# Recurrence of an encoder layer: order of ScalarE's copies, and the state update in two halves

## The reference

```
b = cumsum(log f); state = exp(b_last) * state + (k * exp(b_last - b))^T v
o = (scores of q and k, decayed, lower triangle) v + (q * exp(b)) state
```

## Time and profile before

| what | value |
|---|---|
| median of 3 runs | 1780.27 us (1780.04 to 1784.52) |
| profiled execution | 1780.42 us |
| its span in the trace | 1778.6 us, mean granted clock 0.991 |
| the eight heads | 283.1 to 657.7 us of the span |
| increments of head 1 to increments of head 2 | 46.84 us |

### The profile page before, as it was taken

How to read it: one execution, slowest core, us unless ns; L and a number is a source line. 1 busy time by engine, 2 the same in 40 slices (tenths; PEclk the granted TensorE clock), 3 DMA queues, 4 the chain that set the end, 5 groups by cost and what they waited for, 6 DMA issues and landing times.

```text
span 1778.6 us, 23518 instructions
## 1 busy us (share of the span) xinstructions
PE 1690.8 (95%) x9625; PEld 840.3 (47%) x9625; DVE 598.2 (34%) x942; ACT 331.8 (19%) x512; POOL 136.8 (8%) x141
## 2 busy tenths in 40 slices
PE   6999999999999999999999999999999999898967
PEld 3444455555555555556555554533333333333323
DVE  5010128888888863100112786300000000000008
ACT  1111112222222221112000220022222121121212
POOL 0000000000000000000000111511111111111100
PEclk9999999999999999999999999999999999999989
DMA  6114101110111001111117006699999999999848
GB/s 222 47 48 165 49 24 36 37 35 26 33 35 35 13 1 50 56 47 36 53 53 290 24 36 247 237 422 422 422 425 422 422 423 421 414 411 405 336 197 354
DMA packets 104986, 330.51 MB, mean 186 GB/s; under 512 B 8496, under 2 KB 64848, under 8 KB 86736
## 3 DMA queue, kind: packets, MB, share of 16 engines
q1 hardware_dynamic: 91520, 291.69, 41.5%
q0 software_dynamic: 13392, 37.77, 5.4%
HBM read 306.88 MB, written 33.55 MB: 191 GB/s over the span
## 4 chain that ended last, share of the span: by engine, by line
PE 77%; DMA 12%; DVE 6%; ACT 2%; issue 2%; SPq 0%; POOL 0%; DVEq 0%; POOLq 0%; ACTq 0%
PE pA L1055 14%; PE pg L679 11%; PE pg L706 9%; PE pg L838 9%; PE pB L1081 6%; PE pB L869 5%; DMA rA<-w_e_gate_up 4%; PE pg L719 2%; PE pB L918 2%; PE pA L918 2%; PE pA L861 2%; DMA rCD<-w_e_gate_up 2%; DMA rEF<-w_e_gate_up 2%; DMA rA<-y_dram 2%; DMA rB<-w_e_gate_up 2%
## 5 line engine op out<-in xcount | busy, mean ns | idle before, releaser
L706 PE MATMUL pg<-rA,hw 128*128 128x384 f32 x768 | 264.5, 493 | 0.7 <-ACT aTr L1191 0.7
L1055 PE MATMUL pA<-rCD,aTr 128*32 128x512 f32 (+2 forms) x720 | 209.1, 600 | 11.1 <-DMA rA<-w_e_gate_up 10.1
L679 PE MATMUL pg<-rEF,rA 128*128 128x512 f32 x448 | 194.7, 596 | 3.1 <-ACT rCD L1170 3.1
L1788 DVE TENSOR_TENSOR rows<-rows,pA 128x256 f32<-128x256 f32 x45 | 18.9, 421 | 530.8 <-ACT rows L1314 530.8
L706 PEld LDWEIGHTS pg<-rA,hw 128*128 128x128 f32 x768 | 140.2, 190 | 86.5 <-ACT aTr L1191 0.9
L838 PE MATMUL pg<-rA,hw 128*128 128x384 f32 x512 | 165.3, 486 | 0.0
L679 PEld LDWEIGHTS pg<-rEF,rA 128*128 128x128 f32 x448 | 85.5, 192 | 109.6 <-issue 109.6
L838 PEld LDWEIGHTS pg<-rA,hw 128*128 128x128 f32 x512 | 97.2, 190 | 67.6
L1055 PE MATMUL pA<-rA,aTr 128*32 128x512 f32 (+2 forms) x384 | 124.2, 606 | 0.3 <-DMA rB<-w_e_gate_up 0.3
L1081 PE MATMUL pB<-rCD,rows 128*32 128x512 f32 (+2 forms) x360 | 106.8, 605 | 2.0 <-DMA rCD<-w_e_down 2.0
L1055 PE MATMUL pA<-rB,aTr 128*32 128x512 f32 (+1 forms) x368 | 106.0, 594 | 2.0 <-DMA rEF<-w_e_gate_up 2.0
(11 more groups left out here) (326 smaller groups left out, 2159.6 us busy)
## 6 DMA issues: line engine op xcount, KB each, us to landing
rCD<-w_e_gate_up SPq DMA_DIRECT2D x21, 2048.0 KB, 30.6
rA<-w_e_gate_up SPq DMA_DIRECT2D x11, 2048.0 KB, 31.3
rB<-w_e_gate_up SPq DMA_DIRECT2D x11, 2048.0 KB, 29.6
ew<-w_e_gate_up SPq DMA_DIRECT2D x11, 2048.0 KB, 33.3
rEF<-w_e_gate_up SPq DMA_DIRECT2D x11, 2048.0 KB, 33.0
rCD<-w_e_down SPq DMA_DIRECT2D x21, 1024.0 KB, 33.0
hw<-w_in SPq DMA_DIRECT2D x40, 512.0 KB, 3.9
rA<-w_e_down SPq DMA_DIRECT2D x11, 1024.0 KB, 31.6
```

The source lines that it names most:

```text
L679: last = mm(big_bank(fill), x1T[:, c, i * P:(i + 1) * P], strip[n % 2][:, c, :], start=(c == 0), stop=(c == KC - 1))
L706: last = mm(pg[:, n * 512:n * 512 + HALF], hw3[m][:, c, :], x1T[:, c, n * HALF:(n + 1) * HALF], start=(c == 0), stop=(c == KC - 1))
L1055: last = mm(gu[n][o:o + w, :], xT[n][:, c, o:o + w], at(gate_up_home(j % NB)[0], gate_up_home(j % NB)[1] + c * F, [[2 * D, 2], [1, F]]), s ...
L1788: v.tensor_tensor(hid[n], silu_g[n], gu[n][:, F:2 * F], ALU.mult).then_inc(h_ready, 1)
```

## The change

The transposes and the increments get semaphores of their own (`kt_filled`, `inc_filled`), raised after 4 of 8 tiles and after 8, so that `FILLS` falls from 11 to 9. The decayed keys, the eviction of the transposes and the states are each split in a forward and a backward half. In ScalarE's queue the middle and near copies move ahead of the far ones, and all of them ahead of evict 4.

```diff
-FILLS = 11
+FILLS = 9
...
 def k_transposed():
-    pe.wait_ge(ke_ready, 2 * h + 1)
     for s in range(8):
+        if s % 4 == 0:
+            pe.wait_ge(ke_ready, 3 * h + (s // 4 + 1))
...
-    last.then_inc(hg_filled, 1)
+        if s % 4 == 3:
+            last.then_inc(kt_filled, 1)
 def increments():
-    pe.wait_ge(ke_evicted, h + 1)
     for s in range(8):
+        if s % 4 == 0:
+            pe.wait_ge(ke_evicted, 2 * h + (s // 4 + 1))
...
+        if s % 4 == 3:
+            last.then_inc(inc_filled, 1)
...
 # ScalarE, one head
-for x in range(5): evict(x)
+for x in range(4): evict(x)
 sc.wait_ge(hg_filled, h * FILLS + LEVELS)
 ... middle copies
-sc.wait_ge(hg_filled, h * FILLS + (LEVELS + 1))
-... far copies
 sc.wait_ge(hg_used, h * USES + USES)
 sc.wait_ge(mid_taken, 2 * h + 2)
 ... near copies
-sc.wait_ge(hg_filled, h * FILLS + 9)
-fn(keT, slabs(pair[0][:, :], 8), ACT.Copy).then_inc(ke_evicted, 1)
+sc.wait_ge(hg_filled, h * FILLS + (LEVELS + 1))
+... far copies
+evict(4)
+for a in range(2):
+    half = slice(4 * a * P, 4 * (a + 1) * P)
+    sc.wait_ge(kt_filled, h * 2 + (a + 1))
+    fn(keT[:, 4 * a:4 * a + 4, :], slabs(pair[0][:, half], 4), ACT.Copy).then_inc(ke_evicted, 1)
...
 # VectorE, one head
-v.tensor_tensor(hv("S", 2), hv("S", 2), hv("k", 2), ALU.mult).then_inc(ke_ready, 1)
+for a in range(2):
+    o = slice(a * T, (a + 1) * T)
+    v.tensor_tensor(hv("S", 2)[:, o], hv("S", 2)[:, o], hv("k", 2)[:, o], ALU.mult).then_inc(ke_ready, 1)
...
-ve.wait_ge(hg_filled, h * FILLS + 10)
-corners = [[4 * P, 2], [3 * P, 2], [1, P]]
-link(v.tensor_copy(at(ew, 8 * P, corners), at(pair[1], 0, corners)))
-for s in (1, 2, 5, 6):
+for a in range(2):
+    ve.wait_ge(inc_filled, h * 2 + (a + 1))
+    ends = [[3 * P, 2], [1, P]]
+    link(v.tensor_copy(at(ew, (8 + 4 * a) * P, ends), at(pair[1], 4 * a * P, ends)))
+    for s in (4 * a + 1, 4 * a + 2):
```

More of the change, by code:

```diff
@@ L409, in build @@
         ke_evicted = sem("k_transposed_in_sbuf")
+        kt_filled = sem("k_transposed_in_psum")
+        inc_filled = sem("state_increments_in_psum")
         far_taken = sem("far_scores_in_sbuf")
@@ L788, in increments @@
                                   start=True, stop=True)
-                    last.then_inc(hg_filled, 1)
+                        if s % 4 == 3:
+                            last.then_inc(inc_filled, 1)
                 def outputs():
                     buf = start(10)
-                    pe.wait_ge(ke_ready, 2 * h + 2)
+                    pe.wait_ge(ke_ready, 3 * h + 3)
                     pe.wait_ge(st_ready, h + 1)
@@ L1204, in head @@
                 sc.wait_ge(cur_taken, h + 1)
-                for x in range(5):
-                    evict(x)
                 def scores_out(src, w, g, to):
@@ L1210, in scores_out @@
                               slabs(src[g * w:(g + 1) * w, 0:NT * w], NT), ACT.Copy)
+                for x in range(4):
+                    evict(x)
                 sc.wait_ge(hg_filled, h * FILLS + LEVELS)
@@ L1214, in head @@
                     scores_out(pair[(LEVELS - 1) % 2], HB, g, g).then_inc(mid_taken, 1)
-                sc.wait_ge(hg_filled, h * FILLS + (LEVELS + 1))
-                for g in range(2):
-                    scores_out(pair[LEVELS % 2], HB, g, 1 - g).then_inc(far_taken, 1)
                 sc.wait_ge(hg_used, h * USES + USES)
@@ L1221, in head @@
                     scores_out(near, QB, g, g).then_inc(near_taken, 1)
-                sc.wait_ge(hg_filled, h * FILLS + 9)
-                fn(keT, slabs(pair[0][:, :], 8), ACT.Copy).then_inc(ke_evicted, 1)
+                sc.wait_ge(hg_filled, h * FILLS + (LEVELS + 1))
+                for g in range(2):
+                    scores_out(pair[LEVELS % 2], HB, g, 1 - g).then_inc(far_taken, 1)
+                evict(4)
[3 more added lines that the diff above has]
+                    fn(keT[:, 4 * a:4 * a + 4, :], slabs(pair[0][:, half], 4), ACT.Copy).then_inc(ke_evicted, 1)
                 evict(5)
@@ L1226, in head @@
                     clear_suffixes()
-                sc.wait_ge(hg_filled, h * FILLS + 11)
+                sc.wait_ge(hg_filled, h * FILLS + FILLS)
                 fn(o_tok[:, :, bass.ds(h * DK, DK)].rearrange("p (a b) k -> p a b k", a=2),
@@ L1521, in head @@
                         ve.wait_ge(hg_used, h * USES + (j + 1))
-                v.tensor_tensor(hv("S", 2), hv("S", 2), hv("k", 2), ALU.mult).then_inc(ke_ready, 1)
-                ve.wait_ge(ke_ready, h * 2 + 1)
+                for a in range(2):
+                    o = slice(a * T, (a + 1) * T)
+                    v.tensor_tensor(hv("S", 2)[:, o], hv("S", 2)[:, o], hv("k", 2)[:, o], ALU.mult).then_inc(ke_ready, 1)
+                ve.wait_ge(ke_ready, h * 3 + 2)
                 v.tensor_tensor(slabs(hv("k", 2), 2), at(rEF, OFF["q"], [[0, 2], [1, T]]),
                                 slabs(hv("P", 2), 2), ALU.mult).then_inc(ke_ready, 1)
-                ve.wait_ge(hg_filled, h * FILLS + 10)
-                corners = [[4 * P, 2], [3 * P, 2], [1, P]]
-                link(v.tensor_copy(at(ew, 8 * P, corners), at(pair[1], 0, corners)))
-                for s in (1, 2, 5, 6):
[L1531 to L1537, removed]
+                for a in range(2):
[3 more added lines that the diff above has]
+                    for s in (4 * a + 1, 4 * a + 2):
+                        i = FWD_TILES[s] if s < 4 else BWD_TILES[s - 4]
+                        edge = i * P + P - 1 if s < 4 else T + i * P
+                        last = v.scalar_tensor_tensor(out=states[:, s, :], in0=states[:, s - 1, :],
+                                                      scalar=hv("P", 2)[:, edge:edge + 1],
+                                                      in1=pair[1][:, s * P:(s + 1) * P], op0=ALU.mult, op1=ALU.add)
+                        if s < 6:
+                            link(last)
                 last.then_inc(st_ready, 1)
```

## The result

The changed kernel takes 1772.32 us (median of 5 runs, 1770.77 to 1774.3), against 1780.27 for the kernel before in the same comparison (5 runs, 1779.96 to 1784.52). The medians differ by 7.95 us. The ratio, which goes by all of the runs, is 0.9949, with an interval of 0.9939 to 0.996: 9.1 us faster, between 7.1 and 10.9. The profiled execution took 1770.77 us, with a span of 1768.9. The sum of the prediction was 10.2 us and 1770.2 for a profiled execution.

The account below looks back on a forecast made before the run. TensorE was taken to bound the kernel (77% of the chain), with some 3 us of each 46.84 us head in waits. 7 x 1.37 + 0.57 = 10.2 us off 1780.42 gave 1770.2 profiled, 1770.1 median; range 1766.5 to 1776.5.

Parts of the forecast that it names:

- The circle: Between heads: L1491 waits for the outputs and starts the next head, so earlier outputs shorten a head equally, 1.37 us.
- Keys: Transposes to increments: keys evicted earlier let increments follow the products without a wait, saving 0.60 us (0.52 to 0.70).
- States: Increments to outputs: the forward half of the states overlaps the backward increments, saving 0.77 us a head.
- Edits costed at nothing: Split decayed keys, TensorE's two added waits and evict 4 behind the far copies: each taken to cost or gain 0.
- VectorE's cover behind the outputs: VectorE's idle time before L1491, waiting for the outputs: shrinks from 1.24 to 0.95 us and holds.
- Only the eviction gains: Rival: states still end with the whole increments; a head saves 0.60, the last nothing; 1776 us; chance 0.09, shared.
- The new waits cost more: Rival: TensorE's waits inside transposes and increments cost 0.76 each, more than the gain; 1782 us; chance 0.08, including something unseen.
- Issue stays: Rival: TensorE's wait ahead of the outputs is its own issue and stays; 1776 us; chance 0.09, shared.
- The dearer half: Rival: a half of VectorE's copy and states takes 1.44 us, not 1.20; 6.1 us gained, 1774.3; chance 0.05.
- everything behind the heads shifts and gives nothing back: After the last outputs: later work starts from their end on TensorE's queue, so all 10.2 us reach the whole time.

## Why the prediction was right

*The circle.* L1491 did wait for the outputs in each head, and the head became shorter by what the outputs were earlier: 45.43 against the 45.5 predicted.

*Keys.* 0.60 was reckoned for increments that follow the products without a wait; it was 0.68. TensorE's overlap with the last product was taken too small: the increments start 0.17 ahead of its end (403.80 + 1.46 = 405.26 against 405.09), where 0.09 was put in.

*States.* 0.77 was reckoned, 0.72 measured (4.51 to 3.79). A copy of 256 columns takes 0.42, as interpolated, and a half 1.19 against 1.20. What came out longer is the step from the forward half to the backward one: 1.31 us from copy to copy, not 1.23, though the backward increments are done by 405.09 + 1.95 = 407.04, and the copy starts at 407.49. VectorE stands idle 0.12 us ahead of it instead of 0.03. In the last head, which stands behind VectorE's loop, the same two copies are 1.23 apart. So the hand-over is dearer inside the loop; no run shows why. The first copy, 1.09 behind the increments' start and not 1.14, made up for part of it. And only 0.62 of the 0.72 is the overlap of states and increments, as the states alone show; 0.10 comes from increments that are no longer held, and belongs to the earlier keys.

The two errors cancel, and that is luck: 0.08 more for the keys, 0.05 less for the states, 1.41 a head in place of 1.37. In the last head 0.70 came in place of 0.57, since its outputs follow 0.10 behind the states and not 0.20, before as after. The wait that stays ahead of the outputs is 0.55, not 0.4: the products beside it start 1.78 behind the increments' start, not 1.89, for the first matmul is no longer the long one.

*Edits costed at nothing.* The split keys were worth nothing, shown by the run with whole keys. TensorE's waits cost nothing, shown with 12 more of them. (The price from which they would have eaten the gain is not 0.69 a wait, as the rival has it, but 0.64 over all heads: 10.2 us over 16 waits.) Evict 4 started as its product ended, behind the far copies, with 0.48 to spare. VectorE's cover behind the outputs was predicted to shrink from 1.24 to 0.95; it is 1.17.

*The rivals.* "Only the eviction gains" falls with the halves alone, worth 0.62 a head. "The new waits cost more" falls with the wait ahead of each tile. "Issue stays" falls with the 0.20 between states and outputs, in heads 1 to 6 of every trace. The dearer half falls with the rows: a state follows the copy within 0.04 us, two take 0.73, and a head saves 1.41, not 0.86. That is against the rule of the Trainium skill that was weighed ("VectorE: DVE Perf Modes", section "The DRAIN you can't avoid"), by which a pause of 0.16 would stand there: the measurement decides. The same section adds that an operation which is not held starts earlier, without a size, and so leaves room for what the rows show. The profiled execution took 1770.77, against 1774 by the rule; the median, 1772.32, lies between the two sums and would not have told them apart.

*Where it missed.* It treated order and eviction in halves as one saving and did not see that either alone gives 0.50 or 0.53 of 0.68. It took it that everything behind the heads shifts and gives nothing back. The median came out 2.2 us above 1770.1, so 7.95 us of 10.35 arrived. In the traces this lies in the part behind the heads (1121.7 to 1124.7), of which the execution underlying the sum was among the shortest (1121.0). That term of the sum is not confirmed.

## What to carry to other kernels

When a loop's stages close a circle over several engines, find the instruction that starts the next round and reckon each edit by how much earlier it comes; the sum over rounds was within 2% of the shift of the last outputs here, in part because two errors cancelled, and the whole time gained less than that shift. An eviction stands behind whatever its queue holds: moving small copies into time in which their engine waits anyway, or splitting the eviction, works on the same wait, and one of them alone took about two thirds of it (0.50 or 0.53 of 0.78 us, the held start counted in). Once the tail is shorter, look again at where the filler work stands: moving two steps of it was worth nearly as much again as the change (1.29 us a head), and half of that without it.

## What the hardware showed that was not expected

A group of these matmuls that starts right behind a wait is up to 0.10 us longer: its first matmul takes 0.37 us where otherwise 0.275 is the rule. (In head 0, outside TensorE's loop, it takes 0.35.) The increments' durations in the kernel before (smallest, median, largest, in ns):

```profile
L787 PE MATMUL pB<-rB,ew x128: 272/275/372, 314.9 to 651.7; 128*128 x96, 128*128 128x128 f32 x32
```

and in the changed one:

```profile
L792 PE MATMUL pB<-rB,ew x128: 272/275/276, 314.4 to 642.1; 128*128 x96, 128*128 128x128 f32 x32
```

The outputs show the same behind the wait for VectorE's states, in both kernels: 0.37 in heads 1 to 6, 0.35 in heads 0 and 7. The long one is also there with the order alone, where the trace names no wait ahead of the matmul but its weight load began only with it, at 405.82. So it marks a start that was barely late. In the changed kernel the increments' weights load from 404.77, 0.32 ahead of their matmul. The likely reason is thus that in a held group they are no longer loaded beside the matmul in front; no run here separates that from the wait itself.
